# Value products of two query tiles in one accumulation in the second model's attention

## The reference

```python
def diff_attend(q, k, v, lam):
    s = jnp.einsum('bqhcd,bkhcd->bchqk', q, k).astype(jnp.float32) * (ATT_HEAD_DIM ** -0.5)
    p = jax.nn.softmax(s, axis=-1)
    a = p[:, 0] - lam * p[:, 1]
    return jnp.einsum('bhqk,bkhe->bqhe', a.astype(v.dtype), v)
```

## Time and profile before

| | us |
|---|---|
| median of 3 runs | 3138.54 |
| lowest and highest run | 3131.16, 3141.36 |
| the profiled execution | 3143.51 |
| its span, first to last instruction | 3141.7 |
| mean granted TensorE clock, share of full | 0.984 |

### The profile page before, as it was taken

The page is one execution under the profiler, slowest core; times in us unless marked ns, Lnnn a source line. Parts: engine busy times, 40 slices in busy tenths (PEclk is TensorE's granted clock), DMA queues, the critical chain, the costliest instruction groups (busy, mean ns, idle before and its releaser), DMA issues.

```text
span 3141.7 us, 35319 instructions
## 1 busy us (share of the span) xinstructions
PE 3024.4 (96%) x13820; PEld 2267.1 (72%) x13820; DVE 1194.7 (38%) x2238; ACT 782.2 (25%) x1699; POOL 556.2 (18%) x542
## 2 busy tenths in 40 slices
PE   8999999999999999999999899999999999999998
PEld 6766778887865545555558688888787666678887
DVE  1244232213236554646443443242336555541000
ACT  1012121211013315565620120010113355540000
POOL 0000110002300002122234334443300111110100
PEclk9999999999999899999999999999999999999999
DMA  6455334442336222222212122222321332334342
GB/s 235 146 216 202 120 126 155 147 155 99 108 116 233 81 96 107 95 94 108 81 67 94 67 76 85 91 84 91 97 94 54 111 105 104 106 125 147 135 158 96
DMA packets 65181, 369.77 MB, mean 118 GB/s; under 512 B 6074, under 2 KB 21498, under 8 KB 22672
## 3 DMA queue, kind: packets, MB, share of 16 engines
q1 hardware_dynamic: 48768, 334.60, 29.5%
q10 hardware_dynamic: 15296, 29.56, 2.9%
q0 software_dynamic: 976, 3.63, 0.3%
HBM read 362.30 MB, written 1.28 MB: 116 GB/s over the span
## 4 chain that ended last, share of the span: by engine, by line
PE 92%; DVE 5%; ACT 2%; issue 1%; DMA 0%; POOL 0%; DVEq 0%; ACTq 0%; POOLq 0%
PE PB L1152 13%; PE PB L349 11%; PE PB L467 10%; PE PB L393 9%; PE PB L1000 7%; PE PA L467 6%; PE PB L893 6%; PE PB L1133 5%; PE PS L467 5%; PE PB L1069 4%; PE PB L1166 3%; PE PA L1235 2%; PE PA L1204 1%; PE PA L1218 1%; PE PB L371 1%; ACT work L1574 1%
## 5 line engine op out<-in xcount | busy, mean ns | idle before, releaser
L1152 PE MATMUL PB<-H,ring 128*128 128x512 f32 (+1 forms) x1024 | 429.2, 567 | 0.0
L1152 PEld LDWEIGHTS PB<-H,ring 128*128 128x128 f32 x1024 | 192.4, 191 | 185.8 <-issue 180.4
L393 PE MATMUL PB<-work,ring 128*128 128x256 f32 x1280 | 276.9, 379 | 0.0
L393 PEld LDWEIGHTS PB<-work,ring 128*128 128x128 f32 x1280 | 243.2, 190 | 33.1
L349 PE MATMUL PB<-H,ring 128*128 128x256 f32 x960 | 215.7, 388 | 10.4 <-ACT H L1505 7.5
L349 PEld LDWEIGHTS PB<-H,ring 128*128 128x128 f32 x960 | 187.3, 196 | 39.1 <-issue 12.3
L1000 PE MATMUL PB<-H,ring 128*128 128x256 f32 x992 | 214.3, 379 | 0.0
L1000 PEld LDWEIGHTS PB<-H,ring 128*128 128x128 f32 x992 | 188.5, 190 | 25.6
L2230 DVE SCALAR_TENSOR_TENSOR work<-PB,par,work 128x510 f32<-128x510 f32 (+3 forms) x256 | 181.6, 713 | 24.1 <-ACT work L1616 17.3
L893 PE MATMUL PB<-H,ring 128*128 128x256 f32 (+1 forms) x640 | 179.3, 435 | 1.5 <-ACT mod L1393 0.9
L1133 PE MATMUL PB<-H,ring 128*128 128x512 f32 (+1 forms) x512 | 175.5, 493 | 0.0
(11 more groups left out here) (328 smaller groups left out, 4387.2 us busy)
## 6 DMA issues: line engine op xcount, KB each, us to landing
ring<-stream SPq DMA_DIRECT2D x315, 1024.0 KB, 4.8
sums<-cs_rows ACTq DMA_DIRECT2D x16, 1024.0 KB, 4.7
sums<-cs_rows ACTq DMA_DIRECT2D x16, 512.0 KB, 3.8
work<-work ACTq DMA_DIRECT2D x16, 256.0 KB, 4.4
work<-scratch POOLq DMA_DIRECT2D x1, 2560.0 KB, 13.8
X<-xT SPq DMA_DIRECT2D x2, 1024.0 KB, 15.0
out<-H SPq DMA_DIRECT2D x1, 1024.0 KB, 4.8
con<-consts SPq DMA_DIRECT2D x1, 652.0 KB, 17.7
```

The costliest lines, as they stand in the source:

```text
L393: mm = pe.matmul(PB[:, pair, t, 0:T], ring[:, c % SLOTS, k, t * P:(t + 1) * P], rhs(KT * part + k), start=(part == 0 and k == 0), stop=(pa ...
L1152: mm = pe.matmul(PB[:, pair, t, 0:Tc], ring[:, c % SLOTS, k, t * P:(t + 1) * P], H[:, k, 0:Tc], start=(k == 0), stop=(k == KT - 1))
```

## The change

`values2` now takes a pair p, that is, units 2p and 2p+1: it reads the transposed probabilities of both tiles as one moving operand of 256 columns and writes PA[1], columns 0 to 255. It runs in the even steps from 4 on, behind the fill: `values2(u // 2 - 2)`. AT_T holds two buffers of pairs in place of two of units. Transposes of even units stay in PA[0], which nothing else uses now, and wait for `w_turned` of the unit two before; those of odd units go to PA[1], which they share with the pair's result, and wait for `w_out_read` of the pair before. `out2` copies a pair (128x256) and has moved to the head of ACT's odd steps from 5 on, ahead of `exps2`. `w_out` and `w_out_read` count 16 to a layer.

```diff
-            "w_probs": 32, "w_turned": 32, "w_turns": 32, "w_out_read": 32, "w_out": 32, "w_max": 32,
+            "w_probs": 32, "w_turned": 32, "w_turns": 32, "w_out_read": 16, "w_out": 16, "w_max": 32,
...
-        AT_T = [area(L_TMP + 2048 + 512 * i, 4, P) for i in range(2)]
+        AT_T = [area(L_TMP + 2048 + 1024 * i, 4, 2, P) for i in range(2)]
...
-                    if u >= 2:
-                        pe.wait_ge(sem("w_out_read"), LAYER["w_out_read"] * la + u - 1)
+                    if u % 2 == 0 and u:
+                        pe.wait_ge(sem("w_turned"), LAYER["w_turned"] * la + u - 1)
+                    elif u >= 3:
+                        pe.wait_ge(sem("w_out_read"), LAYER["w_out_read"] * la + u // 2)
...
-                def values2(u):
-                    h, qt, k0, nk = us[u]
+                def values2(p):
+                    h, _, k0, nk = us[2 * p]
                     n = nk // P
-                    pe.wait_ge(sem("w_turned"), LAYER["w_turned"] * la + u + 1)
+                    pe.wait_ge(sem("w_turned"), LAYER["w_turned"] * la + 2 * p + 2)
                     for i in range(n):
-                        mm = pe.matmul(PA[u % 2][:, 0:P], LV[:, k0 // P + i, h * P:(h + 1) * P],
-                                       AT_T[u % 2][:, i, :], start=(i == 0), stop=(i == n - 1))
+                        mm = pe.matmul(PA[1][:, 0:2 * P], LV[:, k0 // P + i, h * P:(h + 1) * P],
+                                       AT_T[p % 2][:, i, :, :], start=(i == 0), stop=(i == n - 1))
                     mm.then_inc(sem("w_out"), 1)
...
-                    if u >= 3:
-                        values2(u - 3)
+                    if u >= 4 and u % 2 == 0:
+                        values2(u // 2 - 2)
...
-                def out2(u):
-                    h, qt, k0, nk = us[u]
-                    act.wait_ge(sem("w_out"), LAYER["w_out"] * la + u + 1)
-                    copy(LQ[:, h, qt * P:(qt + 1) * P], PA[u % 2][:, 0:P], ACT.Copy)\
+                def out2(p):
+                    h, qt, _, _ = us[2 * p]
+                    act.wait_ge(sem("w_out"), LAYER["w_out"] * la + p + 1)
+                    copy(LQ[:, h, qt * P:(qt + 2) * P], PA[1][:, 0:2 * P], ACT.Copy)\
                         .then_inc(sem("w_out_read"), 1)
 
-                for u in range(len(us) + 3):
+                for u in range(len(us) + 4):
                     held.finish(ada_second)
+                    if u >= 5 and u % 2:
+                        out2((u - 5) // 2)
                     if u < len(us):
                         exps2(u)
                         beside(attention_fill(la)[u], ga_out)
-                    if u >= 3:
-                        out2(u - 3)
...
-                    if u >= 2:
-                        v.wait_ge(sem("w_out"), LAYER["w_out"] * la + u - 1)
-                    vec.tensor_copy(AT_T[b][:, 0:n, :], PA[b][:, 0:nk].rearrange("p (a b) -> p a b", a=n))\
+                    if u >= 4:
+                        v.wait_ge(sem("w_out"), LAYER["w_out"] * la + u // 2 - 1)
+                    vec.tensor_copy(AT_T[u // 2 % 2][:, 0:n, b, :], PA[b][:, 0:nk].rearrange("p (a b) -> p a b", a=n))\
                         .then_inc(sem("w_turned"), 1)
```

## The result

The kernel after takes **3154.4 us** (median) where the kernel before took 3138.8: ratio **1.0050, 95% interval 1.0038 to 1.0061**. One of its seven executions took 10782.7 us and is left out of the ratio; the median of the other six is 3153.3. The kernel is slower, and the whole interval lies above 0.3%. The forecast was 3147 with a range to 3157: the sign and the mechanism hold, the size was short by 6 to 7 us. The prediction gave 0.45 to a loss of more than 0.3% and 0.51 to no more than that.

A forecast was written before the change was run, and what follows sets the result against it. PE, 92% of the chain, was taken to bound the kernel, with DVE nearly as full in layer 0. 6.2 + 0.9 + 1.6 = +8.7 us on the profiled 3143.5 gave 3152, less 5.0 for the median 3147; range 3137 to 3157.

The forecast's parts named there:

- The bank wait: Layer 0, full pairs with ada: the even step's chunk waits for DVE to empty its bank; 8.06 against 7.46, +0.60 us.
- a free gate: The gate: a chunk can't enter bank pair 0 until 0.62 us after DVE starts evacuating the one before.
- The ledger of layer 0: Layer 0's steps, costs and savings of the merged blocks listed step by step, together +6.2 us.
- PE's busy time to fall by some us while its idle time grows more: A sign that was to show the forecast right: PE less busy by some us, its idle time up by more.
- The ends: Stage ends: last odd transposes wait for ACT's pair copy, last block is wider; +0.9 us in layer 0, +1.6 in layer 1.
- Copies and layer 1's cycle: Pair copies on ACT and DVE taken as 0, DVE's with up to 3 us loss; layer 1's GA cycle net 0.
- rival B: Clock falls to half in layer 1's last units or among short units; 6.55 us on top, 3154; chance 0.20.
- the 6 to 8 and 1 to 2: A sign of being right: layer 0's stage 6 to 8 us longer, layer 1's 1 to 2, mostly at its end.

The follow-up runs named there:

- e2: The changed kernel with the pair's products moved ahead of the ada or GA chunk in even steps; median 3139.6 us, ratio to before 1.0004.
- e3: The changed kernel with layer 0's ada chunks taking the two banks of pair 0 in turn; 3146.9 us.
- e8: The changed kernel with the edits of e2 and e5 together; median 3139.9 us, ratio to before 1.0005.
- e6: The kernel before with each unit's value products moved ahead of the ada or GA chunk of the same step; 3132.6 us.
- e11: The changed kernel with the odd transposes of layer 0's units 25, 27 and 29 done five times over; median 3146.2 us, ratio to before 1.0026.
- e10: The kernel before with ada chunks taking turns in the two banks of pair 0; 3130.6 us.
- e12: The kernel of e9 with the transposes of layer 0's units 25 to 29 done three times over; median 3132.8 us, ratio to before 0.9975.
- e4: The changed kernel with the pair's products still bunched in the even step, but as two accumulations of 128 columns each; 3156.5 us.
- e5: The changed kernel with only the last odd transposes of each stage put into PA[0]; 3154.1 us.
- e9: The same kernel as e6, executed again for an interval; median 3134.7 us, ratio to before 0.9978.

## Why the prediction was right, and where it was short

**The bank wait: right.** Forecast 8.06 us for two full units, measured 3.72 + 4.33 = 8.05, which is 0.57 over the 7.48 before (forecast 0.60), with L887 0.63 behind L1914. e2 (order) and e3 (bank) each remove it, and the even distance becomes 3.84 or 3.83.

**The ledger of layer 0: right after the clock is taken off.** To the last maximum the kernel lost 7.79; 1.69 of it is a stretch at half clock in step 12 (22.30 us, where e3, whose clock was full there, has 20.61). That leaves 6.10 against 6.2. By step: 6, 8, 10 and 14, +2.2 (2.4); 4 and 12, +0.84 and +0.93 (0.87 each); 16 and 18, +1.0 (1.2); 20, +0.55 (0.43); 22 and 24, +0.52 (0.6); 28, +0.03 (-0.1). e8 shows why it could not have been a gain even with a free gate. In that order, with the clock full, the paired kernel still needs 156.25 where the single one (e6) needs 152.08. In odd steps DVE paces and the missing block wins nothing. In GA steps PE paces and the block is twice as long: 19.42 against 18.59 at step 4.

The prediction also wanted PE's busy time to fall by some us while its idle time grows more. Busy time by window from the first maximum of layer 0 to the last, before and after:

```profile
911.09:1065.26 154.17, 145.19 (x911) 75.64 (x904) 93.74 (x230) 48.99 (x161) 0.00 (x0) 1.00 0.53 197
905.87:1067.83 161.96, 145.04 (x822) 70.47 (x814) 93.61 (x231) 47.59 (x147) 0.00 (x0) 0.99 0.50 188
```

Idle time grew by 7.9 us. Busy time fell by only 0.15, since the stretch at half clock in step 12 took back some 1.7 of what the merged blocks save; over the whole stages, ends included, it even rose, by 1.0 and 1.2.

**The ends: right in kind; in layer 0 too small for the clock that was assumed.** Layer 0's +0.9 was meant for an end at half clock, and there it came to +2.1 (8.32 against 6.23). At full clock the tail is 6.50 (e3, e11) against 5.49 (e10, e12): +1.0. In layer 1, e4's 10.04 less 2 x 0.06 for its narrow blocks is 9.92, against 8.08: +1.8, forecast 1.6. The shared PA[1] is 0.6 to 0.7 of it in layer 1 (e5, e8); in layer 0 it is 0.7 at half clock (e5) and 0.1 at full (e8).

**Copies and layer 1's cycle: right.** DVE's interleaved copy took 0.68, ACT's pair copy 0.38; layer 1 shifted by 0.04 up to its last maximum.

With the clock full throughout, these make 6.10 + 1.0 + 0.04 + 1.8 = 9.0 against the forecast sum of 8.7.

**The step that failed is rival B's place and price.** The text gave the clock one place behind layer 1 or among the short units, all or nothing, at 6.55. Behind layer 1 nothing fell. It fell in step 12 (1.7), in layer 1's last but one block (11.18 - 9.92 = 1.3), and it cost 1.1 more than before in layer 0's tail (8.32 - 6.50, less 6.23 - 5.49): 4.0 us in three small pieces. Forecast and rival B were not alternatives; a part of B came on top. With 0.5 outside the stages this makes 13.5 us, where the medians differ by 15.6 (14.5 with the six executions). The other 1 to 2 are open: executions of either kernel vary by 8 to 13 us, and the profiles show one each. By the same pieces the stages grew by 9.9 and 3.1, outside the 6 to 8 and 1 to 2 that were to show the prediction right.

**Luck.** The text reached 3152 for the profiled execution before it subtracted 5.0 for the median, and the profiled execution of the change took 3151.8. That is chance: the stages and what lies behind them cost 13.5 there, and the stretch ahead of layer 0, with the same code, gave 5.2 back. That the median stayed inside the range is owed to the room left in it for rival B and the copies, not to the sum.

Of the sentences on the Trainium skill: the Trainium skill's Perfetto Trace Analysis (Matmuls) wants independent groups to rotate through PSUM banks. The chunks in two banks (e3) gain 0.5 us a pair where the gate is last and nothing where it is not (e10). The same section of the Trainium skill says "Larger matmuls are more efficient"; here that is worth 0.06 us for eight (e4). The Trainium skill's TensorE: Matmul & The Clock Gate (Part 1) says that activity releases the throttle. e11 agrees, and e3, with 2.15 us of work in 4.22 at full clock, shows that this alone doesn't tell where the clock falls.

## What to carry to other kernels

Merging two small pieces of work into one saves their fixed cost, and also moves the work: ask in which step each piece stood, who paced that step, and which engine must have passed where before the merged block may start. Here 0.22 us a pair was to be saved, and 0.57 was paid because the block landed behind a bank that another engine empties late. Before you widen anything, try the free edit, the order of independent blocks on a full engine: it took the bank wait away in the paired kernel, and on the kernel before it shortened the stage by 1.8 us (the whole ratio there, 0.9978, holds more than the edit is shown to give). And compare stages and distances, not totals: where the low clock fell moved the totals by as much as the edits did.

## What the runs showed of the hardware

- The granted clock falls in places that repeat. In two executions of the change the GA unit of step 12 took 22.30 us and the projection 13.91; e4, e5 and e11, which keep its steps there, have 22.26 to 22.30 for that unit. A small edit elsewhere moves them: e3 had its fall in step 4 (21.31 against 19.62) and none in step 12.
- The same kernel can have the fall behind layer 0 or not (e6 7.36, e9 13.92), and the stretch to the next stage is then 1267.4 or 1275.6 us long: 8.2 us, more than the whole structural effect of most edits here.
- The same code ahead of layer 0 took 904.8 to 911.3 us up to the first maximum. At 15 to 32 us the granted clock was 0.80 in before, 0.90 in e6 and 1.00 in after.
- Adding work to PE went with a kernel 7 to 8 us shorter (e11); the same on another order is undecided (e12). What decides the clock isn't settled by these runs.
